# A two-block transformer in split float32 on one core: the stationary operands moved by 128 and by 448 bytes within the on-chip memory

## The chip, the cores and the metric

One core of one Trainium2 chip runs the program. The metric is the device time of one execution in microseconds, as the median of three runs.

## The reference, cut to what matters

Two blocks run one after the other on 256 tokens of width 1024, all in float32. The first block has two layers with neighbourhood attention and differential attention; the second has two layers, each of two SwiGLU networks around a mixer (pooling in the first layer, block attention in the second), and is modulated by vectors `c_silu @ ada_w`.

```python
for l in range(DEPTH):                         # first block
    h = rmsnorm(x, norm_g[l])
    proj = h @ w_in[l]                         # 256x1024 @ 1024x4096
    ...                                        # two kinds of attention
    x = x + y @ w_out[l]                       # 256x1024 @ 1024x1024
...
def swiglu(h, w_in, w_out):                    # four times in the second block
    gu = h @ w_in                              # 256x1024 @ 1024x5632
    g, u = jnp.split(gu, 2, axis=-1)
    return (jax.nn.silu(g) * u) @ w_out        # 256x2816 @ 2816x1024
```

Nearly all arithmetic is in such products of 256 tokens with a large weight matrix.

## The kernel before

**Products.** Weights arrive in units of 128 partitions x 2048 floats, by DMA from the SP queue into `raw` (six buffers). ScalarE copies each unit to `w_hi` (four buffers) in the type fp32r, which holds fewer bits, and VectorE or GpSimd writes the rest, `raw - w_hi`, to `w_lo`, which lies over `raw`. The activations are split likewise, into `h_hi` and `h_lo`, `yn_hi` and `yn_lo`, or `a_hi` and `a_lo`. A product is then three sums in the same PSUM bank: hi by hi (line 1848), lo by hi (line 1853), hi by lo (line 1861). In each matmul the activations are the stationary operand, a 128x128 tile loaded by a weight-load instruction of its own (PEld in the profile), and the weights are the moving operand, 128x512. Every matmul has its own weight load; no stationary tile is used twice in a row. `half_step` issues them, four matmuls of each kind per unit of 128 tokens:

```python
pe.matmul(bank(b), hi[:, k_in_lhs + k, tok], wh[:, k, c * 512:(c + 1) * 512],
          start=start and k == 0, stop=False)
```

A stationary row is 128 floats, 512 bytes, in each partition, and it begins at the tensor's start plus a multiple of 512 bytes (`k` steps by 1024 bytes, the half `tok` by 512). A moving row is 2048 bytes and begins at the start of `w_hi` or `w_lo` plus a multiple of 2048. So the start address of the tensor alone, modulo 512, says where in a 512-byte stretch every row of it begins.

**Placement.** The function `sb` takes the buffers one behind the other: each begins where the one before it in the program text ends. Buffers entered into a scope of their own (`one`, `early`, `two`, `three`, `four`) give their place back at the end of that scope, and the next scope begins at the same address. The order is: `raw`/`w_lo`, `w_hi`, `ada_raw`, `ada_acc`, `parts` (all of sizes that are multiples of 512 bytes), then `fold`, then `x`, `hn`, `h_hi`, `h_lo`, `row`, `ident` (again multiples of 512), then the small constants `gcols` to `trig_w`, and at the end the scopes.

`fold` is a block of zeros and ones with which `fold_sums` (line 1878) adds partial sums of the modulation vectors; it has 224 floats, 896 bytes. `subc` and `lamt` hold constants of the first block's attention, and `q_scale` four scales in the second block's attention; each has 64 bytes.

**Order of the work.** Each engine's instructions are written out by hand in program order, with semaphores between the engines. The placement of buffers decides no order.

Of the kernel before, what the change touches and what calls it, by code (L numbers as in the profile page):

```python
# [27 lines left out]
P = 128  # L28
D = 1024
T = 256  # L30
NT = T // P
KC = D // P
DEPTH = 2
# [6 lines left out]
NH, DH = 8, 128  # L40
# [10 lines left out]
QUAD = 32  # L51
# [146 lines left out]
def program(nc, known, x_in, w_in, w_out, ffn_in, ffn_out, pool_w, w_kv, w_q, w_o, ada_w, kv_ada_w,  # L198
# [56 lines left out]
    with ExitStack() as ctx:  # L255
# [3 lines left out]
        def sb(name, shape, dt=F32, where=None):  # L259
            return (where or ctx).enter_context(nc.sbuf_tensor(name, shape, dt))  # L260
# [6 lines left out]
        ada_raw = sb("ada_raw", [P, ADA_RING, 2, 512])  # L267
        ada_acc = sb("ada_acc", [P, 512])
        parts = sb("parts", [P, 2, 4, D // QUAD])
        fold = sb("fold", [P, 2 * P - QUAD])  # L270
        x = sb("x", [P, NT, D])
        hn = sb("hn", [P, NT, D])
        h_hi = sb("h_hi", [P, KC, T], F32R)
# [5 lines left out]
        mods = sb("mods", [P, N_VEC, KC])  # L279
        mod_lines = sb("mod_lines", [KC, 2, P])  # L280
        ccol = sb("ccol", [P, 3, KC])
        subc = sb("subc", [P, DEPTH, KC])
        poolc = sb("poolc", [P, KC])
        lamr = sb("lamr", [P, DEPTH, 4, DH_NA])
        lamt = sb("lamt", [P, DEPTH, 8])
        stat = sb("stat", [P, 64])
        minus_half = sb("minus_half", [P, 2 * NH])
        qk_norm = sb("qk_norm", [P, 2, DH])
        trig = sb("trig", [P, NT, 2, DH // 2])

        q_scale = sb("q_scale", [P, NT, NH])
        trig_w = sb("trig_w", [P, 2, NT, 4, DH // 2])

        pool_gate = trig_w.rearrange("p w t i d -> p (w t i d)")
# [5 lines left out]
        with ExitStack() as one:  # L300
            qT = {b: sb(f"q{b}T", [P, 4, T], where=one) for b in "ab"}
            kT = {b: sb(f"k{b}T", [P, 4, T], where=one) for b in "ab"}
            vv = {b: sb(f"v{b}", [P, NT, 512], where=one) for b in "ab"}
            gg = {b: sb(f"g{b}", [P, NT, 512], where=one) for b in "ab"}
            lg1 = sb("lg1", [P, 2, NT, T], where=one)
            pr1 = sb("pr1", [P, 4, NT, T], where=one)
            pT1 = sb("pT1", [P, 2, NT, T], where=one)
            bias1 = sb("bias1", [P, BIASES, NT, T], where=one)
            yn_hi = sb("yn_hi", [P, 4, T], F32R, one)
            yn_lo = sb("yn_lo", [P, 4, T], F32R, one)  # L310
        with ExitStack() as early:

            pool_rows = sb("pool_rows", [P, 2, D], where=early)
            bands = sb("bands", [P, 4, 3, P], where=early)
# [7 lines left out]
        with ExitStack() as four:  # L322
            q2T = sb("q2T", [P, NH, T], where=four)
            qk = sb("qk", [P, NT, D], where=four)
            rot = sb("rot", [P, NT, D], where=four)
            pr2 = sb("pr2", [P, 2, 2 * 512], where=four)
            pT2 = sb("pT2", [P, 2, 2 * 512], where=four)
            mask = sb("mask", [P, 3 * P], where=four)
            cross = sb("cross", [P, 512], where=four)

        ps = ctx.enter_context(nc.psum_tensor("ps", [P, 8, 512], F32))

# [2043 lines left out]
```

## Time and profile before

| | us |
|---|---|
| median of three runs (lowest, highest) | 1211.58 (1211.28, 1212.04) |
| the profiled execution's own time | 1211.91 |
| its span, first to last instruction | 1210.0 |
| PE (TensorE matmul) busy | 1196.2 |
| PEld (TensorE weight load) busy | 970.0 |
| DVE (VectorE) busy | 824.2 |
| ACT (ScalarE) busy | 586.5 |
| POOL (GpSimd) busy | 560.6 |

The ends of matmuls are modelled in the profile, so consecutive ones overlap, and the busy share of PE says little of its pace. The pace is read from the distance between the starts of matmuls: a row of the timeline names how many instructions of one line it merges, so the difference of two rows' starts, divided by the number of matmuls between, is the start-to-start time of one. It is called the gap below.

### The profile page before, as it was taken

Reading aid. Unit: us, or ns where it says so; the run is one execution under the profiler, and the core shown is the slowest. Engines: PE = TensorE matmul, PEld = TensorE weight load, DVE = VectorE, ACT = ScalarE, POOL = GpSimd, SP = SyncE. Lnnn points to the kernel's source line nnn. Section 1 sums busy time; section 2 is a strip of 40 time slices with the busy share of each in tenths; the row PEclk is TensorE's granted clock in tenths of the full one; section 3 lists DMA queues with packets and bytes.
Section 4 is the critical chain, followed back from the end, with each engine's and each line's share of the span. In section 5 each row is a group of like instructions: output and inputs, shape, how many; then the busy total and the mean of one; then the engine's idle time right before and its main releaser. Section 6 shows DMA issues by size and latency. Waiting matters only on the chain.

```text
span 1210.0 us, 15186 instructions
## 1 busy us (share of the span) xinstructions
PE 1196.2 (99%) x5656; PEld 970.0 (80%) x5656; DVE 824.2 (68%) x1140; ACT 586.5 (48%) x764; POOL 560.6 (46%) x418
## 2 busy tenths in 40 slices
PE   9999999999999999999999999999999999999998
PEld 6788887887788878888887878888888887888886
DVE  6895468855796887678769666797782665644423
ACT  5556554665644443554334267443342665443440
POOL 1466334664363552635445127665351563445360
PEclk9999999999999999999999999999999999999999
DMA  9976379746798898459888658799874434775550
GB/s 353 347 274 233 108 251 331 285 141 202 246 329 303 292 336 317 157 196 335 286 313 308 249 190 278 249 332 307 295 294 142 170 133 157 261 240 189 198 191 35
DMA packets 183224, 297.92 MB, mean 246 GB/s; under 512 B 8368, under 2 KB 100208, under 8 KB 183152
## 3 DMA queue, kind: packets, MB, share of 16 engines
q1 hardware_dynamic: 177696, 284.82, 67.7%
q10 hardware_dynamic: 5456, 12.13, 3.0%
q8 instruction: 46, 0.75, 0.3%
q14 instruction: 26, 0.21, 0.1%
HBM read 295.84 MB, written 1.08 MB: 245 GB/s over the span
## 4 chain that ended last, share of the span: by engine, by line
PE 90%; DVE 6%; ACT 2%; issue 1%; DMA 0%; POOL 0%; ACTq 0%; DVEq 0%
PE ps L1848 27%; PE ps L1861 27%; PE ps L1853 27%; PE ps L1945 2%; PE ps L2119 2%; PE ps L2003 1%; PE ps L2031 1%; DVE w_lo L1182 1%; PE ps L2019 1%; DVE ps L1166 1%; PE ps L2042 1%; PE ps L1991 1%; ACT w_hi L646 0%; PE ps L1878 0%; DMA gcols<-norm_cols 0%
## 5 line engine op out<-in xcount | busy, mean ns | idle before, releaser
L515 POOL TENSOR_TENSOR w_lo<-raw,w_hi 128x512 fp32r<-128x512 f32 x348 | 481.7, 1416 | 448.8 <-ACT w_hi L646 448.8
L646 ACT ACTIVATE w_hi<-raw 128x2048 fp32r<-128x2048 f32 x188 | 354.3, 1909 | 106.0 <-PE ps L1861 70.7
L1848 PE MATMUL ps<-w_hi,h_hi 128*128 128x512 f32 x1120 | 315.9, 403 | 0.8 <-issue 0.8
L1861 PE MATMUL ps<-w_lo,h_hi 128*128 128x512 f32 x1120 | 306.4, 395 | 0.2
L1853 PE MATMUL ps<-w_hi,h_lo 128*128 128x512 f32 x1120 | 306.0, 395 | 0.0
L1182 DVE TENSOR_TENSOR w_lo<-raw,w_hi 128x2048 fp32r<-128x2048 f32 x96 | 225.9, 2356 | 109.5 <-ACT w_hi L646 107.3
L1861 PEld LDWEIGHTS ps<-w_lo,h_hi 128*128 128x128 f32 x1120 | 210.1, 188 | 51.6 <-DVE w_lo L1182 1.7
L1853 PEld LDWEIGHTS ps<-w_hi,h_lo 128*128 128x128 f32 x1120 | 210.9, 188 | 49.6
L1848 PEld LDWEIGHTS ps<-w_hi,h_hi 128*128 128x128 f32 x1120 | 202.4, 189 | 47.8 <-issue 6.8
L1166 DVE SCALAR_TENSOR_TENSOR ps<-ada_raw,ccol,ps 128x512 f32<-128x512 f32 x240 | 181.0, 754 | 7.5 <-DMA ada_raw<-ada_w 0.8
L919 ACT ACTIVATE a_hi<-ps 128x512 fp32r<-128x512 f32 x44 | 26.3, 599 | 163.2 <-PE ps L2119 163.2
L506 POOL TENSOR_TENSOR stat<-stat,minus_half 128x1 f32<-128x1 f32 (+3 forms) x25 | 29.1, 1164 | 155.0 <-DVE stat L1218 119.4
L1848 PE MATMUL ps<-w_hi,a_hi 128*128 128x512 f32 x348 | 96.1, 398 | 0.0
L1853 PE MATMUL ps<-w_hi,a_lo 128*128 128x512 f32 x348 | 95.3, 395 | 0.0
L1861 PE MATMUL ps<-w_lo,a_hi 128*128 128x512 f32 x348 | 95.2, 395 | 0.0
L1861 PEld LDWEIGHTS ps<-w_lo,a_hi 128*128 128x128 f32 x348 | 65.4, 188 | 15.8
L1853 PEld LDWEIGHTS ps<-w_hi,a_lo 128*128 128x128 f32 x348 | 65.4, 188 | 15.8
L1848 PEld LDWEIGHTS ps<-w_hi,a_hi 128*128 128x128 f32 x348 | 64.7, 188 | 14.9
L929 ACT ACTIVATE hn<-ps 128x512 f32<-128x512 f32 x44 | 26.3, 598 | 94.7 <-PE ps L1861 94.7
L1536 DVE SCALAR_TENSOR_TENSOR hn<-hn,ps 128x512 f32<-128x512 f32 x44 | 30.1, 685 | 48.5 <-ACT hn L929 48.5
L740 ACT ACTIVATE pr<-lg,stat 128x256 f32<-128x256 f32 x64 | 32.0, 501 | 57.2 <-DVE stat L1326 57.2
L1529 DVE TENSOR_TENSOR a_lo<-ps,a_hi 128x512 fp32r<-128x512 f32 x44 | 30.4, 692 | 35.9 <-ACT a_hi L919 35.0
(200 smaller groups left out, 976.8 us busy)
## 6 DMA issues: line engine op xcount, KB each, us to landing
raw<-ffn_in SPq DMA_DIRECT2D x176, 512.0 KB, 5.6
ada_raw<-ada_w SPq DMA_DIRECT2D x144, 512.0 KB, 6.9
raw<-ffn_out SPq DMA_DIRECT2D x44, 1024.0 KB, 6.3
raw<-w_in SPq DMA_DIRECT2D x31, 1024.0 KB, 8.6
raw<-w_out SPq DMA_DIRECT2D x8, 1024.0 KB, 6.0
ada_raw<-kv_ada_w SPq DMA_DIRECT2D x16, 512.0 KB, 8.6
raw<-w_kv SPq DMA_DIRECT2D x8, 1024.0 KB, 5.6
bias<-na_bias ACTq DMA_DIRECT2D x16, 256.0 KB, 5.2
```

The costliest lines, as they stand in the source:

```text
L506: pool.tensor_tensor(st(at, n), st(at, n), minus_half[:, 0:n], ALU.pow).then_inc(*S.inc("rsqrt_ready", *key))
L515: ins = pool.tensor_tensor(w_lo[:, u % RAW, piece], raw[:, u % RAW, piece], w_hi[:, u % RING, piece].bitcast(F32), ALU.subtract)
L646: act.activation(w_hi[:, u % RING, :], raw[:, u % RAW, :], ACT.Copy).then_inc(*S.inc("w_hi_ready", u))
L740: ins = act.activation(pr1[:, w, t, :], lg1[:, s, t, :], ACT.Exp, bias=st(rs + 2 + t), scale=-1.0, accum_out=st(rs + t))
L919: act.activation(a_hi[:, 2 * g:2 * g + 2, :].rearrange("p k c -> p (k c)"), bank(b), ACT.Copy).then_inc(*S.inc("a_hi_ready", name, g))
L1166: ins = dve.scalar_tensor_tensor(out=into, in0=src, scalar=c, in1=acc, op0=ALU.mult, op1=ALU.add)
L1182: dve.tensor_tensor(w_lo[:, u % RAW, :], raw[:, u % RAW, :], w_hi[:, u % RING, :].bitcast(F32), ALU.subtract).then_inc(*S.inc("w_lo_dve", u))
L1529: dve.tensor_tensor(a_lo[sl].rearrange("p k c -> p (k c)"), bank(b), a_hi[sl].rearrange("p k c -> p (k c)").bitcast(F32), ALU.subtract).th ...
L1536: link(dve.scalar_tensor_tensor(out=ffn_gate, in0=ffn_tanh, scalar=1.0, in1=ps[:, b:b + 2, 0:GC], op0=ALU.add, op1=ALU.mult))
L1848: pe.matmul(bank(b), hi[:, k_in_lhs + k, tok], wh[:, k, c * 512:(c + 1) * 512], start=start and k == 0, stop=False)
L1853: pe.matmul(bank(b), lo[:, k_in_lhs + k, tok], wh[:, k, c * 512:(c + 1) * 512], start=False, stop=False)
L1861: ins = pe.matmul(bank(b), hi[:, k_in_lhs + k, tok], wl[:, k, c * 512:(c + 1) * 512], start=False, stop=stop and k == nk - 1)
```

## The change

`fold` gets 256 floats instead of 224, so it is 128 bytes longer. Its last 32 columns are set to zero with the others and read by nothing. `subc` and `lamt` move from the constants to the end of scope `one`, and `q_scale` to the end of scope `four`. No instruction is added, removed or moved on any engine; one `memset` on GpSimd covers 256 columns instead of 224.

```diff
-        fold = sb("fold", [P, 2 * P - QUAD])
+        fold = sb("fold", [P, 2 * P])
         x = sb("x", [P, NT, D])
...
-        subc = sb("subc", [P, DEPTH, KC])
         poolc = sb("poolc", [P, KC])
         lamr = sb("lamr", [P, DEPTH, 4, DH_NA])
-        lamt = sb("lamt", [P, DEPTH, 8])
...
-        q_scale = sb("q_scale", [P, NT, NH])
         trig_w = sb("trig_w", [P, 2, NT, 4, DH // 2])
...
             yn_lo = sb("yn_lo", [P, 4, T], F32R, one)
+            subc = sb("subc", [P, DEPTH, KC], where=one)
+            lamt = sb("lamt", [P, DEPTH, 8], where=one)
...
             cross = sb("cross", [P, 512], where=four)
+            q_scale = sb("q_scale", [P, NT, NH], where=four)
```

Counted from the start of `raw`, where the weights' rows begin at remainder 0 of 512, the remainders of the other tensors' rows, worked out from the sizes in the program text, are:

| tensors | before | after |
|---|---|---|
| `w_hi`, `w_lo`, `fold`, `parts` | 0 | 0 |
| `h_hi`, `h_lo`, `hn`, `x`, `row`, `ident` | 384 | 0 |
| `yn_hi`, `yn_lo`, `a_hi`, `a_lo` | 64 | 0 |
| all else in the scopes: `qaT` to `pT1`, `bands`, `kvT`, `kvv`, `x_hat01`, `q2T`, `rot`, `pr2`, `pT2` | 64 | 0 |

## Rows read from the trace of the kernel before

**Rows 1.** The page: busy time, granted clock by slice, and the chain of waits
```profile
PE 1196.2 (99%) x5656; PEld 970.0 (80%) x5656; DVE 824.2 (68%) x1140; ACT 586.5 (48%) x764; POOL 560.6 (46%) x418
PEclk9999999999999999999999999999999999999999
PE 90%; DVE 6%; ACT 2%; issue 1%; DMA 0%; POOL 0%; ACTq 0%; DVEq 0%
```

**Rows 2.** The page, costliest groups: one matmul line for each stationary operand
```profile
L1848 PE MATMUL ps<-w_hi,h_hi 128*128 128x512 f32 x1120 | 315.9, 403 | 0.8 <-issue 0.8
L1848 PE MATMUL ps<-w_hi,a_hi 128*128 128x512 f32 x348 | 96.1, 398 | 0.0
```

**Rows 3.** Who waited for whom, PE alone: us in total, times, longest
```profile
PE ps L1958 <- DVE hn L1596: 2.5, 2, 2.3
PE ps L2053 <- DVE row L1462: 1.5, 1, 1.5
```

**Rows 4.** Timeline of PE, `h_hi` and `h_lo` stationary: start, us, instruction
```profile
719.12 1.09 PE L1861 MATMUL ps<-w_lo,h_hi 128*128 128x512 f32 x4
...
747.01 1.09 PE L1861 MATMUL ps<-w_lo,h_hi 128*128 128x512 f32 x4
```

**Rows 5.** Timeline of PE, `h_hi` and `h_lo` stationary, another stretch
```profile
348.88 1.10 PE L1853 MATMUL ps<-w_hi,h_lo 128*128 128x512 f32 x4
...
358.22 1.10 PE L1861 MATMUL ps<-w_lo,h_hi 128*128 128x512 f32 x4
```

**Rows 6.** Timeline of PE, `a_hi` and `a_lo` stationary
```profile
444.57 1.10 PE L1853 MATMUL ps<-w_hi,a_lo 128*128 128x512 f32 x4
...
493.10 1.09 PE L1861 MATMUL ps<-w_lo,a_hi 128*128 128x512 f32 x4
```

**Rows 7.** Line 1853 in these three stretches: duration ns minimum/median/maximum
```profile
L1853 PE MATMUL ps<-w_hi,h_lo x40: 390/392/404, 721.0 to 746.8; 128*128 128x512 f32 x40
L1853 PE MATMUL ps<-w_hi,h_lo x16: 392/395/398, 348.9 to 358.0; 128*128 128x512 f32 x16
L1853 PE MATMUL ps<-w_hi,a_lo x68: 393/396/398, 447.4 to 492.9; 128*128 128x512 f32 x68
```

**Rows 8.** Timeline of PE and PEld side by side
```profile
480.97 1.10 PE L1853 MATMUL ps<-w_hi,a_lo 128*128 128x512 f32 x4
481.67 0.89 PEld L1861 LDWEIGHTS ps<-w_lo,a_hi 128*128 128x128 f32 x4
481.90 1.09 PE L1861 MATMUL ps<-w_lo,a_hi 128*128 128x512 f32 x4
```

**Rows 9.** Scores of the last attention, timeline, then the line's durations
```profile
989.07 1.89 PE L2201 MATMUL ps<-kvT,q2T 128*128 128x256 f32 x8
L2201 PE MATMUL ps<-kvT,q2T x32: 271/327/382, 967.4 to 990.6; 128*128 128x128 f32 x16, 128*128 128x256 f32 x16
```

**Rows 10.** Timeline of PE, the pool product, moving rows of 256 columns
```profile
510.80 0.28 PE L2163 MATMUL ps<-w_hi,h_lo 128*128 128x256 f32 x1
...
511.99 0.28 PE L2164 MATMUL ps<-w_lo,h_hi 128*128 128x256 f32 x1
```

**Rows 11.** Matmul groups of 128 columns: busy us, mean ns
```profile
L2119 PE MATMUL ps<-ident,hn 128*128 128x128 f32 x176 | 26.5, 273 | 0.8 <-DVE hn L1540 0.8
L2019 PE MATMUL ps<-ident,pr 128*128 128x128 f32 x96 | 13.1, 272 | 0.0
L2222 PE MATMUL ps<-kvv,pT 128*128 128x128 f32 x48 | 6.1, 276 | 0.3 <-ACT pT L718 0.3
```

**Rows 12.** The line of `bands`: duration ns minimum/median/maximum
```profile
L1958 PE MATMUL ps<-bands,hn x48: 270/275/579, 494.0 to 509.2; 128*128 128x128 f32 x48
```

**Rows 13.** VectorE's splits of activations: duration ns minimum/median/maximum
```profile
L1242 DVE TENSOR_TENSOR h_lo<-ps,h_hi x36: 685/692/693, 136.1 to 1027.9; 128x512 fp32r<-128x512 f32 x36
L1529 DVE TENSOR_TENSOR a_lo<-ps,a_hi x44: 691/691/694, 333.8 to 1150.8; 128x512 fp32r<-128x512 f32 x44
```

**Rows 14.** Timeline of POOL at the start
```profile
0.78 0.28 POOL L501 MEMSET fold<- 128x224 f32 x1
8.05 1.29 POOL L526 TENSOR_TENSOR w_lo<-raw,w_hi 128x512 fp32r<-128x512 f32 x1 [6.99 <-ACT w_hi L799]
```

## The prediction

> **What bounds the kernel now.** I read the page first. PE is busy for 99% of the span, the granted clock is full in every slice, which is 2.4 GHz, and the chain of waits lies on PE for 90% of its length [rows 1]. The reader should not stop at the 99%, since ends of matmuls are modelled; the waits of PE answer better: the longest two kinds come to 2.5 and 1.5 us in 1210 [rows 3]. So what PE's next instruction waits for is, nearly always, PE. The costliest groups then say which instructions: the products with 512 moving columns [rows 2]. Three kinds for each of two operands, 3 x 1120 with `h` and 3 x 348 with `a`; the lines of `yn` add 3 x 32 and the last step 12 with `a`, so there are 3360 with `h` and 1152 with `a` or `yn`, 4512 in all.
>
> Next the gap, from the timeline. With `h` stationary there are 30 groups of four matmuls between the two rows, 27.89 us, which makes 27.89/120 = 232.4 ns [rows 4]. In another stretch of the same operands 10 groups lie between, 9.34/40 = 233.5 ns [rows 5]. With `a` it is 52 groups, 48.53/208 = 233.3 ns [rows 6]. So 3360 x 232.4 + 1152 x 233.3 = 1050 us, or 87% of the span, are one number times a count, and the change touches nothing but where the stationary rows of these 4512 matmuls begin. A nanosecond on the gap is 4.5 us on the kernel.
>
> **What the gap is made of.** 512 columns at 2.4 GHz are 213 ns. The score matmuls of 256 columns in plain float32 stream as long as that: eight in 1.89 us, the last of 0.38, so (1.89 - 0.38)/7 = 216 ns each [rows 9]. They have a weight load each as well, and they pay nothing for it. The large products pay 16 to 17 ns more. The load for the next matmul begins beside the start of the one before: the loads of line 1861 begin at 481.67, while the matmul they precede by one starts at 481.90 [rows 8], which is one gap of 0.23 us. Both operands are then read at once. The pool product, 256 columns in fp32r, has a gap of (511.99 - 510.80)/10 = 119 ns where its streaming is 107 [rows 10]: again an excess, of 12 ns. I read this as a collision of the two reads, which appears where the moving rows are read at the full rate of fp32r.
>
> Whether the address matters for it is the whole question. For it: at remainder 384 the durations of one line spread from 390 to 404 ns, in the other stretch from 392 to 398, at remainder 64 from 393 to 398 [rows 7]. Duration less gap is constant for matmuls of one shape; with `a` it is (393 + 398)/2 - 233.3 = 162.2. So single gaps are 227.8 to 241.8 with `h`, and 230.8 or 235.8 by turns with `a`. Nothing that is computed differs between them; they depend on how the two reads meet, and the set of levels differs between the two remainders. Against it: the means differ by only 0.9 ns, and one of the two `h` stretches has the mean of `a`.
>
> **The change part by part.** The longer `fold` costs 32/224 of a memset of 0.28 us, 0.04 us on POOL, which waits 6.99 us behind it [rows 14]: nothing. Its zeros are read by no one. The moves of `subc`, `lamt` and `q_scale` change no instruction; their readers and writers do the same work, at another address. VectorE's time for the same split is 692 ns at remainder 384 and 691 at 64 [rows 13], so I put nothing down for other engines. Small matmuls: transposes have equal remainders where `hn` goes with `ident` and unequal ones where `pr` does, with 273 and 272 ns [rows 11]; `bands` against `hn` (unequal) takes 275 and `kvv` against `pT` (equal) 276 [rows 11, 12]. They are bound by the load itself and the change is worth nothing there, within 1 ns x some 1000, 1 us in either direction.
>
> What is left is the gap of the 4512 at equal remainder, with both streams beginning at the same place of a 512-byte stretch within nanoseconds. No large product of this trace has that, so I bound it. From below, the scores, whose remainders are equal (64 and 64): 216 ns, which would save 3360 x 16.4 + 1152 x 17.3 = 75 us. From above, the highest single gap, 241.8 held throughout: 3360 x 9.4 + 1152 x 8.5 = 41 us more. I take a value near the rows of the large products themselves: `a`, whose rows begin 64 bytes from the new place, steps between 230.8 and 235.8, two phases of the same meeting. With equal beginnings every meeting should have the same phase, and I take the lower level, 230.8. The sum: 3360 x (232.4 - 230.8) = 5.4 us and 1152 x (233.3 - 230.8) = 2.9 us, 8.3 us together, taken from 1211.91 of the profiled execution gives 1203.6. That execution was 0.33 above the median, so against the median it is 1203.3. Nothing takes it back: when PE runs 0.7% faster, POOL, ACT and DVE have 46 to 68% busy [rows 1], and they wait for ACT and PE, not the reverse.
>
> The excess of 16 to 17 ns is itself what the trace shows against a rule. The Trainium skill ("SBUF — State Buffer", Who interferes with whom) gives PE two independent read ports, one for the moving operand and one for the weight load, and says that PE never waits on anyone; by that no address could matter and the time would stay at 1211.6, which is the second case below. By the skill ("TensorE: Matmul & The Clock Gate", Back-to-back issue gap) the warm gap is N/2.4 + 2.5, 216 ns at 512 columns; the scores agree with it (216), the large products do not (232 to 233), and the third case is what its value would bring.
>
> **The rivals.**
>
> *No effect.* The collision costs the same wherever the rows begin, and only the mix of phases changes. For it: two remainders 192 bytes apart give means within 0.9 ns; `hn` with `ident` against `pr` with `ident` shows none. Against it: the levels do differ between remainders. If all gaps become 232.4, the time falls by 1152 x 0.9 = 1.0 us to 1210.5; if all become 233.4, it rises by 3360 x 1.0 = 3.4 us to 1215.0.
>
> *The collision goes.* At equal remainder the moving stream, twice as fast as the load, runs away from it and meets it again only where both end. The scores at equal remainder speak for it; against it, they also stream at half the rate, and `bands` against `hn`, unequal and at that rate, shows no excess either, so the rate explains them without the address. Full removal gives 1211.6 - 75 = 1137, and up to 1150 where about a sixth of it is lost again to waits for the weights.
>
> *Slower: the two streams begin on the same place.* The load starts within nanoseconds of a matmul, and at equal remainder both ask for the same place of the stretch from the first byte on; one stands behind the other from the start instead of later. Its place is every one of the 4512 gaps, and its price is the upper level of `a`: 3360 x (235.8 - 232.4) + 1152 x (235.8 - 233.3) = 11.4 + 2.9 = 14.3 us, so 1225.9. It decides as soon as the mean gap is over 233.2, since 0.54 x 4512 = 2.4 us is 0.2% of the time. For it: the meeting at the start is certain here, and `a`, the nearer of the two remainders, has the higher mean. Against it: at 64 bytes the lower level appears as often as the upper.
>
> **How the numbers follow.** The forecast has 0.34, with a range of its own from 1197 to 1209. No effect has 0.34, of which 0.27 within 0.2% and 0.07 above it. The removal has 0.10 and the slower case 0.22. A difference of 0.2%, 2.4 us, is about what a measurement of this kernel can tell from none. So faster is 0.34 + 0.10 = 0.44, the same 0.27, slower 0.07 + 0.22 = 0.29. The range leaves out the removal and the upper half of the slower case: 1190 to 1223.
>
> **What would show each step.** The gap in the stretches of [rows 4] and [rows 6] should be near 231 for both operands, and the spread of line 1853 narrow, 392 to 394 instead of 390 to 404: one phase. If the spread stays wide and the mean in 232.4 to 233.4, the address does not matter. At 395 to 398 throughout it is the slower case; near 378, the removal. The pool product should move with them, from 119 towards 118. Transposes, scores and other engines' durations should stay; if they move, the change does something that I have not seen. The forecast is wrong if the phase is not set by the remainder at all, but by when a stretch begins, as the two stretches with `h` allow.

## The result, and the profile after

| | before | after |
|---|---|---|
| median us (lowest, highest) | 1211.43 (1210.79, 1212.04) | 1193.58 (1192.87, 1193.97) |
| span of the profiled execution | 1210.0 | 1192.1 |
| ratio, 95% interval | | 0.9852, 0.9835 to 0.9869 |

The medians are of four executions each. The change saved 17.9 us, 1.5%, where 8.3 were forecast. The sign and the place were right; the saving is more than twice the forecast. None of the cases had a time near 1193.6: the forecast's own range began at 1197, and that of the removal ended at 1150.

The page of the kernel after shows the other engines' busy time within 1.6 us of before; only PE's moved by more [rows 1]:

```profile
PE 1175.8 (99%) x5656; PEld 968.4 (81%) x5656; DVE 822.8 (69%) x1140; ACT 586.1 (49%) x764; POOL 561.2 (47%) x418
PE 89%; DVE 7%; ACT 2%; issue 1%; POOL 0%; ACTq 0%; DVEq 0%
L1848 PE MATMUL ps<-w_hi,h_hi 128*128 128x512 f32 x1120 | 311.9, 400 | 0.8 <-issue 0.8
L1848 PE MATMUL ps<-w_hi,a_hi 128*128 128x512 f32 x348 | 94.1, 392 | 0.0
```

PE lost 20.4 us of busy time with the same 5656 instructions. The timeline of PE shows it as the gap. With `h` stationary, in the same stretch of the program in which [rows 4] were read:

```profile
708.20 1.18 PE L1848 MATMUL ps<-w_hi,h_hi 128*128 128x512 f32 x4
709.21 1.08 PE L1853 MATMUL ps<-w_hi,h_lo 128*128 128x512 f32 x4
710.13 1.08 PE L1861 MATMUL ps<-w_lo,h_hi 128*128 128x512 f32 x4
711.05 1.07 PE L1848 MATMUL ps<-w_hi,h_hi 128*128 128x512 f32 x4
711.96 1.07 PE L1853 MATMUL ps<-w_hi,h_lo 128*128 128x512 f32 x4
...
736.43 1.07 PE L1853 MATMUL ps<-w_hi,h_lo 128*128 128x512 f32 x4
```

There are 27 groups of four between the last two rows: 24.47/108 = 226.6 ns, against 232.4 in [rows 4]. Ahead of it the stretch has not settled: 709.21 to 711.05 is 1.84/8 = 230 ns. With `a` stationary, 51 groups, 46.25/204 = 226.7 ns, against 233.3 in [rows 6]:

```profile
441.37 1.08 PE L1861 MATMUL ps<-w_lo,a_hi 128*128 128x512 f32 x4
...
487.62 1.07 PE L1861 MATMUL ps<-w_lo,a_hi 128*128 128x512 f32 x4
```

The durations of line 1853 in the same stretches answer to [rows 7]. Where they spread from 390 to 404 at remainder 384 there is now one level with medians of 389 and 390, under the medians of before, 392 to 396; the values up to 398 are from unsettled beginnings:

```profile
L1853 PE MATMUL ps<-w_hi,h_lo x40: 388/389/390, 712.0 to 737.1; 128*128 128x512 f32 x40
L1853 PE MATMUL ps<-w_hi,h_lo x16: 388/390/395, 343.1 to 352.5; 128*128 128x512 f32 x16
L1853 PE MATMUL ps<-w_hi,a_lo x68: 387/389/398, 440.5 to 484.7; 128*128 128x512 f32 x68
```

Worked out from every start in the two traces, gaps between two large products under 262 ns (longer ones follow other work) are on average:

| stationary | count | before | after |
|---|---|---|---|
| `h`, first block | 764 / 765 | 232.3 | 228.4 |
| `h`, second block | 2349 / 2346 | 232.4 | 227.7 |
| `yn` | 86 | 233.2 | 229.0 |
| `a` | 1035 | 233.3 | 227.0 |

The two traces hold the same 5656 matmul records in the same order, so every gap can be set against itself. The 4232 gaps between two large products that were under 262 ns before lost 20.86 us. The span fell by 17.94, so 2.92 us came back: 1.79 us where a small matmul follows a large product, 0.73 between small ones, 0.67 in the longer gaps between large ones and 0.01 at the end, less 0.28 where a large product follows a small matmul. Most of it is waits of PE, after against before [rows 3]:

```profile
PE ps L1958 <- DVE hn L1596: 2.9, 3, 2.3
PE ps L2119 <- DVE hn L1540: 1.4, 2, 0.7
PE ps L1945 <- ACT hn L885: 1.3, 1, 1.3
PE ps L1861 <- DVE w_lo L1182: 0.5, 2, 0.3
```

The first was 2.5 us, the second and third 0.8 and 0.9, the fourth was not in the list. Together they grew by up to 1.9 us. They are waits for work of VectorE and ScalarE that runs beside a product and does not get shorter with it. The third is an example: from the start of line 899 on ScalarE to the first transpose that needs its result it takes 4.94 us in both traces (307.28 to 312.22 before, 305.42 to 310.36 after). It came 1.86 us earlier, and the last large matmuls ahead of those transposes 2.28 us earlier (310.26 and 307.98), so PE waits 0.4 us more.

### The profile page after: what moved, and what is told of

It reads as the page before. It is cut to its first block, busy times and chain, and to the rows that moved or that the text cites. A ratio compares the mean times of both kernels' runs of the same rounds, so it can differ in the third digit from the quotient of the medians.

```text
span 1192.1 us, 15186 instructions
## 1 busy us (share of the span) xinstructions
PE 1175.8 (99%) x5656; PEld 968.4 (81%) x5656; DVE 822.8 (69%) x1140; ACT 586.1 (49%) x764; POOL 561.2 (47%) x418
## 4 chain that ended last, share of the span: by engine, by line
PE 89%; DVE 7%; ACT 2%; issue 1%; POOL 0%; ACTq 0%; DVEq 0%
PE ps L1848 26%; PE ps L1861 26%; PE ps L1853 26%; PE ps L1945 2%; PE ps L2119 2%; PE ps L2003 1%; DVE w_lo L1182 1%; PE ps L2031 1%; PE ps L2019 1%; DVE ps L1166 1%; ACT w_hi L646 1%; PE ps L2042 1%; PE ps L1991 1%; PE ps L2053 1%; PE ps L1878 0%
## 5 line engine op out<-in xcount | busy, mean ns | idle before, releaser
L1848 PE MATMUL ps<-w_hi,h_hi 128*128 128x512 f32 x1120 | 311.9, 400 | 0.8 <-issue 0.8
L1861 PE MATMUL ps<-w_lo,h_hi 128*128 128x512 f32 x1120 | 301.4, 391 | 0.9 <-DVE w_lo L1182 0.5
L1853 PE MATMUL ps<-w_hi,h_lo 128*128 128x512 f32 x1120 | 300.5, 390 | 0.0
```

The source lines that it names most:

```text
L1853: pe.matmul(bank(b), lo[:, k_in_lhs + k, tok], wh[:, k, c * 512:(c + 1) * 512], start=False, stop=False)
L1861: ins = pe.matmul(bank(b), hi[:, k_in_lhs + k, tok], wl[:, k, c * 512:(c + 1) * 512], start=False, stop=stop and k == nk - 1)
```

## The experiments

The layouts below differ from the kernel after in fillers and in the order of small constants; no instruction is added or removed. Where `fold` is back at 224 columns its memset covers 224. Remainders are those of the stationary rows less that of the weights' rows, in bytes.

### Each half alone

```diff
 # only_h: h at 0, scopes back at 64
+        pad_scopes = sb("pad_scopes", [P, 16])
         with ExitStack() as one:
 # only_a: h back at 384, scopes at 0
-        fold = sb("fold", [P, 2 * P])
+        fold = sb("fold", [P, 224])
+        pad_scopes = sb("pad_scopes", [P, 32])
         with ExitStack() as one:
```

> Half of the change: h_hi, h_lo (3360 matmuls) at remainder 0 as after, yn and a (1152) left at 64 as before, by a filler of 64 bytes ahead of the scopes. Theory P (the gap of each product is set by the place of its own stationary row): h at 227.8 ns, a stays at 233.3, time 1193.6 + 1152 x 6.3 ns = about 1200.5. Rival Q (some other buffer's address, or the whole layout, brought the gain): h or a at another gap, time near 1211 or near 1193.6.

> The other half: h_hi, h_lo left at remainder 384, yn and a at 0. Theory P: a at 226.9 ns, h stays at 232.4, time 1211.4 - 6.9 = about 1204.5, and the gains of the two halves add up to the whole within 1 us. Rival Q: no gain, or all of it.

Measured: `only_h` 1200.38 us, ratio 0.9906 (0.9891 to 0.9921), gaps of `h` 227.7 in the second block, of `a` 233.3. `only_a` 1205.15 us, 0.9948 (0.9933 to 0.9962), `h` 232.4, `a` 227.1. The half with `h` is worth 11.2 us and the other 6.4, together 17.6 of the 17.9. In `only_h` the group with `a` reads as before, and the one with `h` as after:

```profile
L1854 PE MATMUL ps<-w_hi,h_lo 128*128 128x512 f32 x1120 | 300.5, 390 | 0.0
L1854 PE MATMUL ps<-w_hi,a_lo 128*128 128x512 f32 x348 | 95.3, 395 | 0.0
```

So each product's gap follows its own stationary rows. The other buffers of the scopes moved together with `a` and `yn`; the series below, in which nothing else moves, show that they are not needed to explain it.

### The whole memory 128 bytes further on

```diff
+        pad_front = sb("pad_front", [P, 32])
         with ExitStack() as in_place:
```

> All buffers, the weights too, 128 bytes further on than after: remainders relative to the weights are 0 as after, absolute ones are other. Theory R (only the distance of stationary and moving row modulo 512 counts): time and gaps as after, 1193.6 within 0.2%. Rival S (the absolute address of the stationary row counts): another gap, since h was 128 bytes lower before and slower; up to 1211.

Measured: 1193.34 us, 0.985 (0.9833 to 0.9866), gaps 227.7 and 227.0. This shift of all addresses changes nothing, and rival S has fallen.

### A series of places in one run

```diff
             warm_up(WARM_UP[0])
+            for at, start, n, step, plain in SWEEP:
+                pe.matmul(bank(ADA_BANK)[:, 0:64], row[:, 0:P], row[:, 0:64], start=True, stop=True)
+                for i in range(REPS):
+                    a = at + step * (i % 4)
+                    lhs, rhs = still[:, a:a + P], moved[:, start + 512 * (i % 2):start + 512 * (i % 2) + n]
+                    ...
+                    pe.matmul(bank(ADA_BANK)[:, 0:n], lhs, rhs, start=True, stop=True)
```

`still` is `h_hi` and `moved` is `h_lo`, set to zero first.

> The kernel after with 33 series of 48 matmuls ahead of its work, on zeros, whose results are thrown away; its time is about 350 us longer and says nothing. Each series has one place of the stationary row relative to the moving row: 0, 32, ... 480 bytes, then 4, 8, 16; then equal places at 64, 256 and 384 and the stationary row at 0 with the moving one at 384; then one stationary tile used again at 0 and 384; 256 columns at 0, 64, 384, the same in plain float32; and last 512 and 128. Theory R: the gap is a function of the difference alone: 226 to 227 at 0, 232.4 at 384, 233.3 at 64, the equal places as 0, the moving row at 384 as stationary at 128. 256 columns: 119 at 384, less at 0. Plain float32: the same at all three. Rival T (single meeting, my reading before the result): a minimum at 0 alone and a flat 232 to 234 elsewhere. Rival U (gradual): the gap changes step by step with the difference, and some place is better than 0.

Each series is one row of the timeline. The first gap of a series, 0.31 us, and the last duration, 0.39, are taken off, and 46 gaps are left. The first three rows are the places 0, 32 and 64; then 192, 256 and 384:

```profile
10.14 11.15 PE L2069 MATMUL ps<-h_lo,h_hi 128*128 128x512 f32 x48
21.27 11.45 PE L2069 MATMUL ps<-h_lo,h_hi 128*128 128x512 f32 x48
32.70 11.44 PE L2069 MATMUL ps<-h_lo,h_hi 128*128 128x512 f32 x48
...
78.37 11.25 PE L2069 MATMUL ps<-h_lo,h_hi 128*128 128x512 f32 x48
...
101.01 11.18 PE L2069 MATMUL ps<-h_lo,h_hi 128*128 128x512 f32 x48
...
146.46 11.39 PE L2069 MATMUL ps<-h_lo,h_hi 128*128 128x512 f32 x48
```

(11.15 - 0.70)/46 is 227.2 ns at 0, 233.7 at 32, 229.3 at 192, 227.8 at 256, 232.4 at 384. The last 24 gaps of each series, from the single starts, give the settled values:

| bytes | 0 | 32 | 64 | 96 | 128 | 160 | 192 | 224 |
|---|---|---|---|---|---|---|---|---|
| ns | 226.7 | 233.3 | 233.3 | 234.2 | 232.1 | 233.3 | 228.9 | 233.3 |
| the same + 256 | 226.7 | 233.3 | 233.3 | 234.2 | 232.1 | 233.3 | 228.9 | 233.3 |

The pattern repeats after 256 bytes. Both tensors moved together to 64, 256 or 384 give 226.7; the moving row alone at 384 gives 232.1, the value of 128, which is theory R. Rival T, my reading ahead of the result, has fallen, since 192 is good as well, and so has U, since the gap does not change gradually. One stationary tile used again and again instead of four in turn gives the same (226.7 at 0, 232.8 at 384), and so do 512 bytes (226.7). With 256 columns the gap is 120.0 at 0, 113.3 at 64 and 118.7 at 384: here equal places are the worst of the three. In plain float32, also with 256 columns, each matmul leaves two records (96 for 48 matmuls), and their starts are 215.8 ns apart at all three places.

### Two layouts at other places

```diff
 # h256_a128: gcols and minus_half (384 bytes) ahead of x, 256 bytes ahead of the scopes
 # h192_a448: gcols (320 bytes) ahead of x, 64 bytes ahead of the scopes
-        fold = sb("fold", [P, 2 * P])
+        fold = sb("fold", [P, 224])
+        gcols = sb("gcols", [P, 10, KC])
+        ...
         x = sb("x", [P, NT, D])
```

> h_hi, h_lo at remainder 256 of 512, yn and a at 128. By the series (period of 256 bytes, theory V): h as at 0, 227.8 ns, a as at 384, 232.2; time 1193.6 + 1152 x 5.2 ns = 1199.6. Rival W (the remainder of 512 must be 0, the series on zeros ahead of the kernel doesn't carry over): h near 232 to 233, time over 1210.

> h at remainder 192, yn and a at 448. Theory V: the series gave 228.9 ns at both, settled after some four matmuls, where remainder 0 takes eight to twelve at a mean of 231 before it settles at 226.7. So a (long stretches) 228.9 against 226.9 at 0, h (stretches of 11 to 47) 229.0 against 227.8: time 1193.6 + 1152 x 1.9 + 3360 x 1.1 ns = about 1199.5, and the first block, whose stretches are of 11, no slower than after. Rival W: 232 to 233 and over 1210.

Measured: `h256_a128` 1199.09 us, 0.9896 (0.9879 to 0.9914), `h` 227.7, `a` 232.5. `h192_a448` 1199.32 us, 0.99 (0.9883 to 0.9918), `h` 229.3, `a` 229.0. Both sums, 1199.6 and 1199.5, were met within about 0.5 us. The series carry over to the kernel, and a remainder of 256 serves `h` as well as 0. One thing in the second expectation failed: in the first block its gap is 229.6, and not under the 228.4 of after.

### Steps of four bytes, fewer columns

The series as above, with 40 matmuls each: 64 places 4 bytes apart in the one, `still[:, a:a + m]` with `m` of 128, 96, 64 and 32 in the other.

> 64 series of 40 matmuls ahead of the kernel's work (on zeros, thrown away), with the stationary row at 0, 4, ... 252 bytes from the moving one. Theory X (blocks of 32 bytes: where the load crosses from one block to the next in step with the stream): steps of 4 bytes change the gap as much as 32 do, no place under 226.7. Rival Y: some place off the multiples of 32 is near 216.

The settled gap is 226.7 at 0, 16, 100, 120, 132, 156 and 240; most places 230 to 233.3; the worst 237.7 at 164. None was under 226.7, so rival Y fell. But 16 bytes had been 233.3 in the series before, and 128 bytes 232.1, here 233.3: some places have two states. Each place ran once here, so the map does not say which others have.

> 16 series of 40 matmuls ahead of the kernel's work, with stationary tiles of 128, 96, 64 and 32 columns at 0, 64, 128 and 192 bytes. Theory Z (the excess over 216 is paid while the load is read beside the stream): it falls in proportion to the columns: at 64 bytes 17.5, 13, 9, 4 ns, at 0 bytes 11, 8, 5.5, 3. Rival: the excess is a cost of the switch between tiles and stays at 11 to 17 whatever the number of columns.

```profile
19.48 9.58 PE L2069 MATMUL ps<-h_lo,h_hi 128*128 128x512 f32 x40
...
57.35 9.37 PE L2069 MATMUL ps<-h_lo,h_hi 128*96 128x512 f32 x40
...
95.06 9.43 PE L2069 MATMUL ps<-h_lo,h_hi 128*64 128x512 f32 x40
...
132.62 9.47 PE L2069 MATMUL ps<-h_lo,h_hi 128*32 128x512 f32 x40
```

The rows are the place 64 with 128, 96, 64 and 32 columns of the stationary tile. Over the last 24 gaps of each series, from the single starts, the settled values in ns are:

| bytes | 128 columns | 96 | 64 | 32 |
|---|---|---|---|---|
| 0 | 226.7 | 230.0 | 230.0 | 231.7 |
| 64 | 233.3 | 228.3 | 231.1 | 231.7 |
| 128 | 232.1 | 231.7 | 231.1 | 231.0 |
| 192 | 228.9 | 233.3 | 228.3 | 231.7 |

The loads themselves got shorter, 188, 161, 134 and 108 ns. Theory Z has fallen: with a quarter of the columns the excess over 215.8 is still 15 to 16 ns at every place. It is not paid column by column while the load is read, as the prediction had it. What a narrower load takes away is the advantage of 0 bytes: 96 columns there are slower than 128. Which place is good depends on the width of the load too, and with 32 columns the four places lie within 0.7 ns.

### Breaks, a version that beats both, and narrower rows

Ahead of each series of 24 matmuls stand one to six small float32 matmuls of `row`, for 18 places.

> Ahead of the kernel's work 18 places of the stationary row (0, 8, 16, 44, 100, 108, 116, 120, 132, 152, 156, 176, 192, 228, 240, 256, 384 and 64 bytes), each six times 24 matmuls, with one to six small float32 matmuls before each series. Settled gaps in the earlier series were 226.7 at 0, 100, 120, 132, 156, 240, 256, and at 16 once 226.7 and once 233.3. Theory V: 0 and 256 settle at 226.7 in all six after some eight gaps at 231, mean about 228; if 100, 120, 132, 156 or 240 settle there in all six and sooner, a layout with that place is faster than after by up to 1 ns x 3360 = 3.4 us. Rival: these places have two states, as 16 has, and their mean over six is over 228.

Mean over the six series, without the first gap of each: 227.7 at 0, 228.0 at 256, 227.3 at 120, 228.0 at 132, 227.8 at 240. At 100 it is 230.2 and at 16 231.1, since four of their six series end at 230 to 233. At 240 three of six end at 228.3, at 192 one of six at 233.3 and the others at 228.9, and 156 bytes settled at 243.3 in five of six. At 120 all six settled at 226.7, three from their second gap on. That place was then built into the kernel:

```diff
-        h_hi = sb("h_hi", [P, KC, T], F32R)
-        h_lo = sb("h_lo", [P, KC, T], F32R)
+        h_both = sb("h_both", [P, 2 * KC * T + 32], F32R)
+        h_hi, h_lo = (h_both[:, 30 + i * KC * T:30 + (i + 1) * KC * T].rearrange("p (k t) -> p k t", k=KC)
+                      for i in range(2))
```

> A version meant to beat after: h_hi, h_lo at 120 bytes from the weights' remainder (in one buffer with a gap in front), all scopes at 256. The series with breaks gave 227.3 ns at 120 against 227.7 at 0, with the same settled 226.7, so 3360 x 0.4 = 1.3 us less than after; where the breaks in the kernel (four 128-column transposes) leave it in the better of its two beginnings each time, 3360 x 1.1 = 3.7 us less. Expected 1190 to 1193. Rival (the place has another, worse state, as 100 and 16 have): h above 228.5 and over 1195.

> The kernel after, once more, beside h120_a256 on the same chip: 1193.5, h 227.9, a 227.0.

Measured side by side: `h120_a256` 1191.31 us (1190.79 to 1191.8, five runs), 0.9834 (0.982 to 0.9847) of before; `after_again` 1193.96 (1192.86 to 1194.17, four runs), 0.9854 (0.984 to 0.9867). The intervals of the ratios overlap, the single times do not. The difference is 2.7 us, and the gap of `h` is 226.9 instead of 227.7 in the second block, 227.4 instead of 228.2 in the first: 3110 x 0.8 = 2.5 us, `a` being at 226.9 in both. The stretch that took three groups to settle in after is settled here from its second group on, in steps of 0.91 us and 0.90:

```profile
706.27 1.17 PE L1850 MATMUL ps<-w_hi,h_both 128*128 128x512 f32 x4
707.28 1.07 PE L1855 MATMUL ps<-w_hi,h_both 128*128 128x512 f32 x4
708.19 1.07 PE L1863 MATMUL ps<-w_lo,h_both 128*128 128x512 f32 x4
709.10 1.07 PE L1850 MATMUL ps<-w_hi,h_both 128*128 128x512 f32 x4
710.00 1.07 PE L1855 MATMUL ps<-w_hi,h_both 128*128 128x512 f32 x4
```

> 30 series of 40 matmuls ahead of the kernel's work: moving rows of 512, 504, 496, 480, 448, 384, 320, 256, 192 and 128 columns, each at 0, 64 and 128 bytes. Settled gaps so far lie on multiples of 6.67 ns (226.67 = 34, 233.33 = 35, 113.33 = 17, 120 = 18) or on simple fractions between two of them. Theory G (a grid): the settled gap falls in steps of 6.67 ns as the columns get fewer, with 512, 504 and 496 columns often on the same step. Rival: it falls evenly, 3.3 ns for 8 columns, and the multiples are chance.

```profile
11.26 9.36 PE L2069 MATMUL ps<-h_lo,h_hi 128*128 128x512 f32 x40
...
39.67 9.33 PE L2069 MATMUL ps<-h_lo,h_hi 128*128 128x504 f32 x40
...
67.88 9.18 PE L2069 MATMUL ps<-h_lo,h_hi 128*128 128x496 f32 x40
```

Settled at 0 bytes: 226.7 with 512 columns and with 504, 223.3 with 496, 216.7 with 480, 202.7 with 448, 173.3 with 384, 146.7 with 320. At 64 bytes: 233.3, 228.9, 220.0, 215.8, 202.3, 173.3, 146.7. At 128 bytes: 232.1, 233.3, 226.7, 220.0, 204.2, 176.0, 146.7. At 256 columns: 120.0, 113.3 and 118.6. So the gap does not fall evenly, which speaks against the rival, but it stops at other values than multiples of 6.67 ns too (215.8, 202.3), which theory G does not have. It is not settled. What is seen is that the three places differ by 4 to 7 ns from 480 columns up and at 256, by 2 to 3 ns at 448 and 384, and not at 320. At 192 and 128 columns all have 111.7.

## Why the prediction was wrong

- **What bounds the kernel**: right. Gap times count gave the time in every layout: the two halves, 256 with 128, and 192 with 448 were foretold within 1 us from gaps alone.
- **"What the gap is made of"**: half right. There is an excess over 216 ns, it depends on the distance between stationary and moving row, and plain float32 has none. The picture of two reads that collide for as long as the load lasts was wrong: with 32 columns instead of 128 the excess is 15 to 16 ns at all four places. The comparison with the scores was misread as well: the eight of [rows 9] are records of four matmuls, since a plain float32 matmul leaves two, so 256 columns take 2 x 216 ns there. That is about a quarter of the pace of fp32r, not half of it.
- **"I take the lower level, 230.8"**: this step failed. One phase for all meetings was right where a stretch has settled, but its level is 226.7, 4 ns under the one taken, and under the lowest single gap that the prediction worked out for its stretches, 227.8. The levels of remainder 64 did not carry over to 0, though only 64 bytes away; between them 32 has 233.3, 16 has two states, and 4 has 232. Taking over a level from an address 64 bytes away was the error. With the measured means the terms are 3360 x 4.5 = 15.1 us and 1152 x 6.2 = 7.1 us, in place of 5.4 and 2.9. Their 22.2 us are a little more than the 20.9 measured, since only 4232 of the 4512 follow another large product at its pace; the others begin a stretch or wait.
- **"Nothing takes it back"**: wrong by 2.9 us of 20.9. Waits of PE for the ends of norms and for `w_lo` grew. The busy shares of 46 to 68% that I argued from say nothing about a chain at the end of a product.
- **Small matmuls, scores, other engines, the longer `fold`**: right. In the kernel after, `hn` with `ident` has 273 ns, `pr` 272, `kvv` with `pT` 277, and the split on VectorE 692 [rows 11, 13]. The memset takes 0.31 us. The pool product did not go towards 118: it stays at (506.99 - 505.80)/10 = 119 ns, as the series show for 256 columns (118.7 at 384, 120.0 at 0):

```profile
505.80 0.28 PE L2163 MATMUL ps<-w_hi,h_lo 128*128 128x256 f32 x1
...
506.99 0.28 PE L2164 MATMUL ps<-w_lo,h_hi 128*128 128x256 f32 x1
```

- **The rivals**: "no effect" fell with the gaps of the timeline. The removal came closest in kind, about a third of the excess gone, but the argument for it, that equal rows meet only at their ends, does not hold: 256 and 120 bytes do as well. The slower case, held to be certain to meet at the start, had the wrong sign.
- By the Trainium skill ("SBUF — State Buffer", Who interferes with whom) PE has two independent read ports and never waits on anyone. The runs do not bear out what the prediction drew from this, that no address could matter: in fp32r the distance of the two rows alone moved the settled gap from 226.7 to 243.3 ns. Whether a read port is what waits, no run shows.

Not settled is what the excess consists of, and why 0, 120 and 256 bytes are good and 64 is not. That the distance sets the gap is shown; the series give the map, not the mechanism.

## What to carry to other kernels

Where one kind of matmul makes up most of the time, read its start-to-start time and compare it with what its columns take at the granted clock; an excess of a few per cent may hang on the distance between the stationary and the moving row, and 64 bytes of filler can be worth 1%. Do not interpolate between addresses: a series of dummy matmuls ahead of the kernel maps many places in one run, and gaps read there, times the counts, gave the kernel's time within 1 us. Run a place more than once, with other work ahead of it, before building on it: 16 bytes gave 226.7 ns in one series and 233.3 in another. And run it with the kernel's own shapes: 0 bytes is best with 512 moving and 128 stationary columns, and not with 256 moving or 96 stationary ones. When a product gets faster, expect its final chain of waits to keep its length.

## What the runs showed of the hardware that was not expected

- The gap of an fp32r matmul with 512 columns and a weight load of its own takes settled values of 226.7 to 237.7 ns in the series of every fourth byte, by the distance of the two rows, and the values at multiples of 32 bytes repeat after 256. It differs between places only 4 bytes apart (226.7 at 0, 232.5 at 4, 230.7 at 8). Moving both operands together changed nothing, in the series and in the kernel. The values at 0 and 64 were the same on the three chips on which series ran.
- Some distances have two or more states (16 bytes: 226.7 or 233.3; 156 bytes: 226.7 or 243.3; 192 bytes: 228.9 or 233.3), which changed with the small matmuls ahead of the series; 0, 120, 132 and 256 bytes ended at 226.7 in all six.
- At distance 0 a series took two to nine more gaps after its first, at 231 to 232 ns on average, to settle, and so again after each break; only one, with both rows at 384 bytes, was settled from its second gap on.
- A narrower weight load does not take the excess away: 15 to 16 ns over 215.8 remain with 32 columns, and at 0 bytes the gap rises from 226.7 with 128 columns to 230.0 with 96. Plain float32 has 215.8 ns between records at 0, 64 and 384 bytes, two records for each matmul of 256 columns.
